# Shared values of layer 1 by one plain fp32 product per chunk in place of three products of split parts

## The reference, cut to what matters

```python
if l == N_A_LAYERS - 1:
    kv = (rmsnorm(x, shared_norm) @ shared_w_kv).reshape(B, S, 2, n_dil, HEAD_DIM)
    shared_k = partial_rope(kv[:, :, 0], cos, sin)
    shared_v = kv[:, :, 1]
```

## Time and profile before

| | us |
|---|---|
| median of 3 runs | 3370.5 |
| lowest, highest | 3369.85, 3378.69 |
| the profiled execution: its own time | 3374.21 |
| its span, first to last instruction | 3372.1 |
| TensorE busy | 3255.9 (97%) |
| DVE busy | 2592.0 (77%) |
| ACT busy | 1621.1 (48%) |
| mean granted TensorE clock | 0.982 |

### The profile page before, as it was taken

How to read it: one execution, slowest core, us unless ns; L and a number is a source line. 1 busy time by engine, 2 the same in 40 slices (tenths; PEclk the granted TensorE clock), 3 DMA queues, 4 the chain that set the end, 5 groups by cost and what they waited for, 6 DMA issues and landing times. The chain is left out here.

```text
span 3372.1 us, 50125 instructions
## 1 busy us (share of the span) xinstructions
PE 3255.9 (97%) x18534; PEld 2908.7 (86%) x18534; DVE 2592.0 (77%) x5275; ACT 1621.1 (48%) x3007; POOL 1071.0 (32%) x666
## 2 busy tenths in 40 slices
PE   7988999999999999999999998999999999999998
PEld 7867899999999888887988876899999998888886
DVE  4764898888857888886377764799888866888886
ACT  4333247676853333334354544237776763333333
POOL 2301363434313454550000001354343322545441
PEclk9988999999999999999999998999999999999999
DMA  5103358888899999994222212348887889999995
GB/s 178 52 19 105 103 171 291 290 301 280 309 322 343 407 399 391 388 398 157 71 82 70 82 45 69 132 134 288 286 311 285 290 321 329 407 405 394 393 393 200
DMA packets 324355, 833.71 MB, mean 247 GB/s; under 512 B 26000, under 2 KB 160656, under 8 KB 320016
## 3 DMA queue, kind: packets, MB, share of 16 engines
q1 hardware_dynamic: 250384, 562.04, 46.5%
q0 software_dynamic: 73728, 268.47, 21.8%
HBM read 721.30 MB, written 109.10 MB: 246 GB/s over the span
## 5 line engine op out<-in xcount | busy, mean ns | idle before, releaser
L1941 ACT ACTIVATE peer_hi<-raw 128x1024 fp32r<-128x1024 f32 x540 | 571.0, 1058 | 660.4 <-PE p_bank L1879 524.8
L2210 DVE TENSOR_TENSOR peer_lo<-raw,peer_hi 128x1024 fp32r<-128x1024 f32 x434 | 531.0, 1224 | 324.1 <-ACT peer_hi L1941 320.0
L1807 POOL DMA_INDIRECT p_grow<-in_u_rows,p_expert x256 | 335.5, 1310 | 691.5 <-DVE p_hid L2218 674.6
L1807 POOL DMA_INDIRECT p_grow<-in_v_rows,p_expert x256 | 400.2, 1563 | 397.2 <-DVE p_acc L2227 361.7
L1879 PE MATMUL p_bank<-peer_hi,p_w_hi 128*128 128x512 f32 x1500 | 462.0, 389 | 0.4 <-DVE peer_lo L2210 0.3
L1879 PE MATMUL p_bank<-peer_lo,p_w_hi 128*128 128x512 f32 x1500 | 461.8, 389 | 0.0
L1879 PE MATMUL p_bank<-peer_hi,p_w_lo 128*128 128x512 f32 x1500 | 461.8, 389 | 0.0
L1829 PE MATMUL p1r_h_ps<-h_hi,peer_hi 128*128 128x384 f32 (+1 forms) x1152 | 399.7, 347 | 15.5 <-ACT p_h_sb L1955 10.6
L1829 PE MATMUL p0r_h_ps<-h_hi,peer_hi 128*128 128x384 f32 (+1 forms) x1152 | 400.3, 347 | 13.6 <-ACT p_h_sb L1955 8.8
L1829 PE MATMUL p0r_h_ps<-h_lo,peer_hi 128*128 128x384 f32 (+1 forms) x1152 | 394.3, 342 | 0.0
L1829 PE MATMUL p0r_h_ps<-h_hi,peer_lo 128*128 128x384 f32 (+1 forms) x1152 | 394.2, 342 | 0.0
(11 more groups left out here) (372 smaller groups left out, 5821.4 us busy)
## 6 DMA issues: line engine op xcount, KB each, us to landing
raw<-in_u SPq DMA_DIRECT2D x256, 512.0 KB
raw<-in_v SPq DMA_DIRECT2D x256, 512.0 KB
hiddens<-p_h_sb SPq DMA_DIRECT2D x256, 192.0 KB
p_w_raw<-hiddens SPq DMA_DIRECT2D x64, 768.0 KB
p_g_sb<-gates SPq DMA_DIRECT2D x64, 768.0 KB
gates<-x SPq DMA_DIRECT2D x12, 2048.0 KB
raw<-in_w_b_mix SPq DMA_DIRECT2D x38, 512.0 KB
raw<-in_w_peer_q SPq DMA_DIRECT2D x32, 512.0 KB
```

The source lines that it names most:

```text
L1807: pool.indirect_dma_start(out=grow[:, g % RG, :], out_offset=None, in_=table, in_offset=bass.IndirectOffsetOnAxis(ap=expert[:, at:at + 1], ...
L1941: act.activation(hi[:, n % NH, :], raw[:, n % NR, :], ACT.Copy).then_inc(hi_ready, 1)
L2210: dve.tensor_tensor(lo[:, m % NH, :], raw[:, m % NR, :], hi[:, m % NH, :].bitcast(F32), ALU.subtract).then_inc(lo_dve, 1)
```

## The change

Weights and tokens of the value stage are no longer split. ACT's scaled copy goes to one plain fp32 tensor `w` (half the space of the two). DVE adds the tokens' two parts into one plain fp32 tensor `near_h`, 8 sums of 128 x 512 at the stage's start, and makes no low parts. ACT spreads `near_h` into one tensor `far_h`, 8 copies in place of 16. Each k chunk of a bank is one matmul of fp32 by fp32 in place of three. SyncE's waits go to ACT's counter `w_ready` in place of DVE's `lo_ready`. Order of loops, tiles, banks, ring and double buffer stay.

```diff
--- before.py
+++ after.py
@@ -131,14 +131,14 @@
     tiles = TT
     NS = KC // SVK
     with Stage(nc, name) as st:
-        w_hi = st.sb("w_hi", [P, 2, KC, cw], F32R)
-        w_lo = st.sb("w_lo", [P, 2, KC, cw], F32R)
-        far_h = [st.sb(f"far{n}", [P, KC, S], F32R) for n in range(2)]
+        w = st.sb("w", [P, 2, KC, cw])
+        near_h = st.sb("near_h", [P, KC, S])
+        far_h = st.sb("far_h", [P, KC, S])
         bank = st.ps("bank", [P, 4, 512])
         w_loaded = [st.sem(f"w_loaded{u}") for u in range(SVP)]
         next_loaded = [st.sem(f"next_loaded{n}") for n in range(AHEAD)]
-        hi_ready, lo_ready, summed, moved, spread = [
-            st.sem(s) for s in ("hi_ready", "lo_ready", "summed", "moved", "spread")]
+        w_ready, whole, summed, moved, spread = [
+            st.sem(s) for s in ("w_ready", "whole", "summed", "moved", "spread")]
 
         def w_at(c, k):
             return shared_piece(raw, c * NS + k // SVK)[:, k % SVK, :]
@@ -147,9 +147,9 @@
             @block.sync
             def _(sp):
                 for p in range(SVP, n_chunks * NS):
-                    sp.wait_ge(lo_ready, (p - SVP + 1) * SVK)
+                    sp.wait_ge(w_ready, (p - SVP + 1) * SVK)
                     sp.dma_start(shared_piece(raw, p), shared_source(w_dram, p)).then_inc(w_loaded[p % SVP], 16)
-                sp.wait_ge(lo_ready, n_chunks * KC)
+                sp.wait_ge(w_ready, n_chunks * KC)
                 for n in range(AHEAD):
                     sp.dma_start(raw[:, AHEAD + n, :].rearrange("p (k f) -> p k f", k=KC), next_w[n])\
                         .then_inc(next_loaded[n], 16)
@@ -166,15 +166,15 @@
                         p = c * NS + k // SVK
                         if k % SVK == 0 and p >= SVP:
                             act.wait_ge(w_loaded[p % SVP], 16 * (p // SVP))
-                        act.activation(w_hi[:, c % 2, k, :], w_at(c, k), ACT.Copy,
-                                       scale=gain(k)).then_inc(hi_ready, 1)
+                        act.activation(w[:, c % 2, k, :], w_at(c, k), ACT.Copy,
+                                       scale=gain(k)).then_inc(w_ready, 1)
                     if c == 1:
 
                         for k in range(KC):
-                            for to, fr in zip(far_h, h):
-                                act.activation(to[:, k, :].rearrange("p (r j) -> p r j", r=DIL),
-                                               fr[:, k, :].bitcast(F32).rearrange("p (j r) -> p r j", r=DIL),
-                                               ACT.Copy).then_inc(spread, 1)
+                            act.wait_ge(whole, k + 1)
+                            act.activation(far_h[:, k, :].rearrange("p (r j) -> p r j", r=DIL),
+                                           near_h[:, k, :].rearrange("p (j r) -> p r j", r=DIL),
+                                           ACT.Copy).then_inc(spread, 1)
 
             @block.tensor
             def _(pe):
@@ -186,29 +186,22 @@
                             pe.wait_ge(moved, n - 3)
                         for k in range(KC):
                             if t == 0:
-                                pe.wait_ge(lo_ready, c * KC + k + 1)
+                                pe.wait_ge(w_ready, c * KC + k + 1)
+                            if n == 0:
+                                pe.wait_ge(whole, k + 1)
                             if t == 0 and c == n_near:
-                                pe.wait_ge(spread, 2 * (k + 1))
-                            for s, (a, b) in enumerate(((0, w_hi), (0, w_lo), (1, w_hi))):
-                                mm = pe.matmul(bank[:, n % 4, 0:cw], (h if c < n_near else far_h)[a][:, k, t * P:(t + 1) * P], b[:, c % 2, k, :],
-                                               start=(k == 0 and s == 0), stop=(k == KC - 1 and s == 2))
+                                pe.wait_ge(spread, k + 1)
+                            mm = pe.matmul(bank[:, n % 4, 0:cw], (near_h if c < n_near else far_h)[:, k, t * P:(t + 1) * P],
+                                           w[:, c % 2, k, :], start=k == 0, stop=k == KC - 1)
                         mm.then_inc(summed, 1)
 
             @block.vector
             def _(dve):
-                def lower(c, k):
-                    dve.wait_ge(hi_ready, c * KC + k + 1)
-                    dve.scalar_tensor_tensor(out=w_lo[:, c % 2, k, :], in0=w_at(c, k), scalar=gain(k),
-                                             in1=w_hi[:, c % 2, k, :].bitcast(F32), op0=ALU.mult,
-                                             op1=ALU.subtract).then_inc(lo_ready, 1)
-
                 for k in range(KC):
-                    lower(0, k)
+                    dve.tensor_tensor(near_h[:, k, :], h[0][:, k, :].bitcast(F32), h[1][:, k, :].bitcast(F32),
+                                      ALU.add).then_inc(whole, 1)
                 for c in range(n_chunks):
                     for t in range(tiles):
-                        if c + 1 < n_chunks:
-                            lower(c + 1, 2 * t)
-                            lower(c + 1, 2 * t + 1)
                         n = c * tiles + t
                         dve.wait_ge(summed, n + 1)
                         dve.tensor_copy(out(t, c), bank[:, n % 4, 0:cw]).then_inc(moved, 1)
```

## The result

| | before | changed |
|---|---|---|
| median, us | 3370.4 | 3397.8 |
| lowest to highest | 3369.9 to 3378.7 (4 runs) | 3392.8 to 3398.8 (4 runs) |
| profiled execution: time, span | 3374.2, 3372.1 | 3398.5, 3396.5 |

The ratio is 1.0073, 95% interval 1.0054 to 1.0091: slower, by less than 1%. The forecast was 3394.0, +23.5 us. One execution of the changed kernel in the second measurement took 11153 us at a mean granted clock of 0.355, and it stands in no ratio and no median of this text.

The account below looks back on a forecast made before the run. The prediction took TensorE's stream of products to bound the value stage. TensorE's +24.1 us and the start's -0.6 us sum to +23.5, which on the median of 3370.5 gives 3394.0 us, range 3387 to 3402.

Parts of the forecast that it names:

- What bounds the stage: Value stage: it lasts as long as TensorE's products; relieving ACT or DVE is worth nothing except before the first matmul.
- TensorE, forecast +24.1 us: Value stage matmuls: 384 plain records at 323 ns, 124.0 us, replace 576 split ones at 173.5 ns, 99.9 us.
- the estimate of four passes in the prediction: Value stage products: a Trainium skill page gives true FP32 four passes through the array, 4 x 160 = 640 ns.
- The weight load is hidden: Plain records of the value stage: a load of about 107 ns fits under a stream of 320 ns.
- rival 1: Value stage matmuls: plain records stream once, the load alone setting 111 ns at 128 columns; total 3339 us, chance 5%.
- The stage's start, forecast -0.6 us: Value stage's start: ACT's first copy and DVE's first sum run side by side, so matmuls start earlier; bounds -0.7 and 0.
- ACT, transfers, hand-over, worth nothing: Value stage and its end: fewer spreading copies and SyncE's earlier wait gain nothing; the hand-over keeps its instructions.
- One pass per record (3339): Value stage matmuls: a plain product takes 347 ns, 192 of them 66.6 us, total 3339 us; chance 5%.
- The 13.5 ns on top of plain records too (3398): Value stage matmuls: plain records pay the split records' extra time, +27.6 us, total 3398 us; chance 15%.
- An exposed load (3435): Value stage matmuls: each record's weight load of 0.107 us adds to its stream, 41 us more, 3435 us; chance 4%.
- A clock that does not hold: Value stage: a long plain stream runs at half clock, records 0.64 us, stage 246 us, total about 3515; chance 3%.
- The sum: Whole kernel: 24.1 - 0.6 = +23.5 us on the median of 3370.5, giving 3394.0 us; chance 73%.

Follow-up runs that it names:

- the second measurement: The changed kernel again, unaltered, against the kernel before, in five more rounds: median 3395.8 us, ratio 1.0065.
- the run with two products: The kernel before with the split product of the tokens' low part by the weights' high part left out: 3343.5 us in one execution.

## Why the prediction was right

- **What bounds the stage.** TensorE's stream alone, after its first matmul. The waits and stretches of the changed kernel show it, and DVE's work put back changed nothing.
- **TensorE, forecast +24.1 us:** from first matmul to the last period's end 101.4 before, 125.6 after, +24.2. The period was taken as 323 ns and is 322.5; the duration as 482 and is 486. The two readings on which it rested, two columns' worth of time per column and a few ns on top, hold at 192 and 384 columns. The product takes 645 ns, where the estimate of four passes in the prediction has 640.
- **The weight load is hidden.** With 384 columns it is: 2.5 ns come on top of the stream. But the prediction read one row wrongly. It took the 111 ns of a 128-column record as 107 for two passes and 4 on top, and the 64-column records as 107 ns apart. That second figure has the group's short first step, 55 ns, in it. Without the first record the trace of the kernel before has 15 records in 1.84 us (the line below), and less the last one's 275 ns that is 1.565/14 = 0.112 us each. So 64 and 128 columns both come some 111.7 ns apart: that is the floor, and the 128-column row told nothing of passes or of what comes on top, as rival 1 said. The durations carried the forecast. Only the periods at 192 and 384 columns, measured after it, show the two passes.

```profile
1771.80 1.84 PE L392 MATMUL ba_o_ps<-dil_v,ba_eT 128*128 128x64 f32 x15
```

- **The stage's start, forecast -0.6 us:** measured -0.46. DVE's first sum took 0.69 us, as forecast; the first matmul starts 0.15 us after its end, which the forecast left out. DVE's sums kept ahead after that: TensorE waits once.
- **ACT, transfers, hand-over, worth nothing:** the hand-over is 2.09 us in both. ACT's spreading ends at 1605.3 in the changed kernel, and the first product with far tokens starts at 1632.5; that such a cover can end is shown by the run with two products, where it cost 3.7 us.
- **The rivals.** One pass per record (3339): no, 384 records at 322.5. The 13.5 ns on top of plain records too (3398): no, 2.5, although the first median of 3397.8 lies exactly there: the profile, not the median, tells the two apart. An exposed load (3435): no. A clock that does not hold: not with plain products, which ran at 1.00 after the first 3.4 us, but this rival's mechanism exists: it struck the split ones at 128 columns.
- **The sum.** 24.2 - 0.46 = +23.7 in the stage, against 23.5 forecast, and two profiles have it there. The medians are coarser: the first measurement's +27.4 holds about 3.7 us that belong to no part of the change, the second gave +22.6. That the forecast lies between them is no finer proof.
- **Left open.** Why a split record has 13.3 ns on top of its stream and a plain one 2.5 for its two passes was not tried, nor whether the floor of 111.7 ns is the weight load.

## What to carry to other kernels

Where TensorE's stream is the bound, compare two ways to multiply by columns streamed per product at the width used, not by the number of instructions: three split fp32 products stream 3 x 384 columns (520 ns with what comes on top), one plain one streams 4 x 384 (645 ns), and the work taken from DVE bought nothing back. The comparison turns round for narrow products (here from 192 columns down), where a record costs at least 111.7 ns, and three of them cost more than two. Don't put narrow split products first after a gap of TensorE; in this stage beginning with wide ones took 192 us off.

## What the runs showed of the hardware that was not expected

- A stream of split 128-column matmuls leaves the clock as it finds it: 0.50 for 367 us when it began with the clock low or about to fall (two kernels, five executions, two of them profiled), 1.00 for 163 us when wide matmuls came first (one execution). The same 128 columns as plain products, streamed twice and as far apart, let the clock rise after 3.4 us.
- At clock 0.50 the periods are less than twice those at the full clock. Whole split matmuls come 320 ns apart, their stream of 384 columns at 1.2 GHz, and 173.3 at 2.4 GHz, 13.3 more than the stream; plain ones 640 and 322.5; records at the floor 213.3 and 111.7.
- A start flag on one piece of a PSUM bank marks the whole bank. The Trainium skill, page "PSUM — Partial Sum Buffer", section The four PSUM rules, states this; the kernels with one flag per bank agree.
